# A head's sample outer products in one burst of four row tiles, and the first output chunk begun ahead of the last head's scores

## What is computed

```python
def _layer(h, pos, S0, ...):
    xn = _rmsnorm(h, norm_g)
    q, k, v, g_r, u, v_g, g_g = split(xn @ w_in)              # 7 x 1024 columns, 8 heads of 128
    q, k = rope(q), rope(k) * 128 ** -0.5
    o, S = retention(q, k, v, S0)    # per token: S = gamma_h * S + k^T v ; o = q S
    o = groupnorm(o) * silu(g_r)
    m = u * spatial_gate(layernorm(v_g)) * silu(g_g)
    return h + concat([o, m]) @ w_out, S, vn
```

## Time and profile before

| | us |
|---|---|
| median of 3 runs | 1172.91 (1171.78 to 1173.85) |
| the profiled execution | 1175.36 |
| span of its slowest core (core 2) | 1173.8 |
| spans of the eight cores | 1166.6 to 1173.8 |
| PE busy in that span | 1136.2 (97%) |
| DVE, POOL, ACT busy | 807.6, 661.8, 640.2 |

### The profile page before, as it was taken

How to read it: one execution, slowest core, us unless ns; L and a number is a source line. 1 busy time by engine, 2 the same in 40 slices (tenths; PEclk the granted TensorE clock), 3 DMA queues, 4 the chain that set the end, 5 groups by cost and what they waited for, 6 DMA issues and landing times.

```text
span 1173.8 us, 27480 instructions; the slowest of 8 cores (1166.6 to 1173.8 us)
## 1 busy us (share of the span) xinstructions
PE 1136.2 (97%) x9302; PEld 646.3 (55%) x9302; DVE 807.6 (69%) x1567; ACT 640.2 (55%) x1142; POOL 661.8 (56%) x696
## 2 busy tenths in 40 slices
PE   5899999999999999999999999999999999999997
PEld 2454456666666665544544445666666666664453
DVE  3864667776776777776574487776776776776864
ACT  4484566555555656524443488555655655663433
POOL 3346356567567666503475785567666666662332
PEclk9999999999999999999999999999999999999999
DMA  9731546456556466756791028256446447556543
GB/s 206 178 99 36 83 93 133 103 92 125 115 90 120 100 116 152 128 170 155 177 208 28 12 40 157 79 100 117 104 99 124 111 86 129 125 119 144 180 182 144
DMA packets 144489, 139.59 MB, mean 119 GB/s; under 512 B 41952, under 2 KB 115424, under 8 KB 144352
## 3 DMA queue, kind: packets, MB, share of 16 engines
q1 hardware_dynamic: 123088, 95.11, 29.0%
q0 software_dynamic: 21120, 42.48, 24.5%
q10 hardware_dynamic: 144, 0.26, 0.1%
HBM read 124.51 MB, written 43.19 MB: 143 GB/s over the span
## 4 chain that ended last, share of the span: by engine, by line
PE 85%; ACT 6%; issue 3%; DMA 3%; DVE 2%; POOL 1%; DVEq 0%; ACTq 0%; POOLq 0%; SPq 0%
PE ps L824 32%; PE ps L702 12%; PE ps L1233 10%; PE ps L868 9%; PE ps L633 5%; PE ps L1175 4%; ACT L483 2%; ACT B_q L483 1%; PE ps L903 1%; PE ps L949 1%; PE ps L1031 1%; PE ps L989 1%; PE ps L952 1%; PE ps L574 1%; DMA h<-hb_51 1%
## 5 line engine op out<-in xcount | busy, mean ns | idle before, releaser
L483 ACT ACTIVATE B_q<-ps 64x512 f32<-64x512 f32 x128 | 75.8, 592 | 98.7 <-DVE A_q L849 62.9
L483 ACT ACT_TABLE_LOAD x73 | 93.7, 1283 | 15.2 <-DVE rs L960 10.1
L840 POOL TENSOR_TENSOR kT_83<-A_k,B_k 128x512 bf16<-128x512 f32 x32 | 40.7, 1272 | 80.4 <-DVE B_k L838 80.4
L483 ACT ACTIVATE sq<-ps 128x512 f32<-128x512 f32 x64 | 38.2, 596 | 45.8 <-PE ps L952 45.0
L958 DVE TENSOR_TENSOR og<-ps,sgr_96 128x512 f32<-128x512 f32 x32 | 22.1, 692 | 59.1 <-ACT sq L483 59.1
L840 POOL TENSOR_TENSOR kT_84<-A_k,B_k 128x512 bf16<-128x512 f32 x32 | 41.1, 1283 | 28.8 <-DVE B_k L838 28.7
L958 DVE TENSOR_TENSOR og<-ps,sgr_97 128x512 f32<-128x512 f32 x32 | 22.1, 692 | 47.1 <-ACT sq L483 47.1
L1233 PE MATMUL ps<-TT,VV 128*128 128x512 bf16 x240 | 54.2, 379 | 0.0
L931 DVE SCALAR_TENSOR_TENSOR S32b<-S32b,ps 128x128 f32<-128x128 f32 x120 | 33.8, 282 | 18.7 <-PE ps L922 17.5
L999 POOL TENSOR_TENSOR VV<-s_100,sgg_99 128x512 bf16<-128x512 f32 x32 | 37.1, 1158 | 16.4 <-DVE kn_s L1063 11.6
L931 DVE SCALAR_TENSOR_TENSOR S32a<-S32a,ps 128x128 f32<-128x128 f32 x120 | 33.9, 282 | 17.8 <-PE ps L922 15.7
(11 more groups left out here) (674 smaller groups left out, 3505.8 us busy)
## 6 DMA issues: line engine op xcount, KB each, us to landing
stt_143<-st SPq DMA_DIRECT2D x16, 512.0 KB, 4.2
stt_142<-st SPq DMA_DIRECT2D x16, 512.0 KB, 4.8
ss_out<-stt_142 SPq DMA_DIRECT2D x16, 512.0 KB, 4.3
ss_out<-stt_143 SPq DMA_DIRECT2D x16, 512.0 KB, 3.7
cats<-catn_94 SPq DMA_DIRECT2D x14, 256.0 KB, 4.2
cats<-catn_95 SPq DMA_DIRECT2D x14, 256.0 KB, 3.4
hb_49<-xp SPq DMA_DIRECT2D x6, 512.0 KB, 4.2
hb_50<-xp SPq DMA_DIRECT2D x6, 512.0 KB, 4.0
```

The source lines that it names most:

```text
L483: P.add("act", lambda e: e.activation(out=out, in_=in_, func=func, **kw), r, w, t_act(n) + (0.2 if "accum_out" in kw else 0), tset=tset)
L840: pool(lambda e: e.tensor_tensor(out=dst[:], in0=A_k[:], in1=B_k[:], op=ALU.add), A_k.k() + B_k.k(), dst.k(), 512)
```

## The change

`s_kv` is no longer called once for each half. It becomes a generator that is begun once for each head, in quarter 2: it takes four banks, issues all four outer products in one operation, and holds back those banks that have not been summed yet, so that `brot` does not hand them out. Its first two sums and the write of half 0 stand in quarter 2, as before; the third stands behind `SC` in quarter 3, the fourth and the write of half 1 behind `OO` in quarter 3. The copy to `stb` becomes a step of its own (`s_stb`), half 0 in quarter 2 and half 1 in quarter 3 behind `s_o` of half 0. Behind the loop, the first four weight pairs of output chunk 0 are put ahead of `SC`, `GM` and `OO` of the last unit, in two banks of `brot` that are held back from these; the last `s_o` moves behind chunk 0's other three pairs and takes a bank of `tbank`.

```diff
@@ class Rot
+                self.items, self.i, self.held = list(items), 0, set()
             def __call__(self):
+                while True:
+                    x = self.items[self.i % len(self.items)]
+                    self.i += 1
+                    if x not in self.held:
+                        return x
@@ s_kv
-        def s_kv(l, h, half):
-            t = stt[half]
-            bs = (brot(), brot())
+        def s_kv(l, h):
+            bs = [brot() for _ in range(4)]
             def mm(e):
-                for j in range(2):
-                    p0 = (half * 2 + j) * 32
-                    r = e.matmul(ps[:, bs[j], :], kn_s[p0:p0 + 32, :], vmask[p0:p0 + 32].rearrange("p b v -> p (b v)"),
+                for j in range(4):
+                    r = e.matmul(ps[:, bs[j], :], kn_s[j * 32:j * 32 + 32, :], vmask[j * 32:j * 32 + 32].rearrange("p b v -> p (b v)"),
                                  start=True, stop=True)
                 return r
-            pe(mm, kn_s.k() + vmask.k(), [bk(b) for b in bs], 1.5 * MM)
+            pe(mm, kn_s.k() + vmask.k(), [bk(b) for b in bs], 2 * MM)
+            brot.held.update(bs)
             for j, b in enumerate(bs):
...
+                t, j0 = stt[j // 2], j % 2 * 4
+                dve((lambda t, j0, b: lambda e: e.scalar_tensor_tensor(
+                    out=t[:, j0:j0 + 4, :], in0=t[:, j0:j0 + 4, :], scalar=_C["gam"][h],
+                    in1=ps[:, b, :].rearrange("p (b v) -> p b v", b=4), op0=ALU.mult, op1=ALU.add))(t, j0, b),
+                    t.k((j0, j0 + 4)), t.k((j0, j0 + 4)) + [bk(b)], 512)
+                brot.held.discard(b)
+                if j % 2:
+                    half = j // 2
+                    dma("sp", ss_out[l, half * 8:half * 8 + 8, h].rearrange("b d v -> d b v"), t[:], t.k(), [("sso", l, h, half)], t.name, 524288)
+                yield
+
+        def s_stb(half):
+            act(stb[:], stt[half][:], AF.Copy, stt[half].k(), stb.k(), 1024)
+
+        def s_o(l, h, half, bank=None):
+            b = (bank or brot)()
@@ o_front
+        def o_front(l, c, a=0, b=7):
+            if a == 0:
+                obanks[c] = (orot(), orot())
+            o_mm(l, c, obanks[c], cat_ap(c), cat_k(c), 128, JO[a:b])
@@ the loop over units
                     SC(l, p)
+                if u.q == 3:
+                    next(kv)
...
                     OO(l, p, pp)
+                if u.q == 3:
+                    next(kv)
...
                 if u.q == 2:
-                    s_kv(l, h, 0)
+                    kv = s_kv(l, h)
+                    for t in range(2):
+                        next(kv)
+                    s_stb(0)
                     if h + 1 < H:
                         w_prep2(l, h + 1)
                 if u.q == 3:
                     s_o(l, h, 0)
-                    s_kv(l, h, 1)
+                    s_stb(1)
@@ behind the loop
+            first = [brot() for _ in range(5)]
+            orot.items, orot.i = first + [b for b in range(6) if b not in first], 0
+            o_front(l, 0, 0, 4)
+            brot.held.update(obanks[0])
             SC(l, p)
             GM(l, p)
             OO(l, p, pp)
-            s_o(l, H - 1, 1)
...
             for c in range(3):
-                o_front(l, c)
+                o_front(l, c, 4 * (c == 0))
+                if c == 0:
+                    s_o(l, H - 1, 1, tbank)
```

More of the change, by code:

```diff
@@ L469, in __init__ @@
             def __init__(self, items):
-                self.items, self.i = list(items), 0
+                self.items, self.i, self.held = list(items), 0, set()
             def __call__(self):
-                x = self.items[self.i % len(self.items)]
-                self.i += 1
-                return x
+                while True:
[3 more added lines that the diff above has]
+                        return x
         def pe(fn, r, w, dur, slack=0.0):
@@ L1188, in build_nc @@
         obanks = {}
-        def o_front(l, c):
-            obanks[c] = (orot(), orot())
-            o_mm(l, c, obanks[c], cat_ap(c), cat_k(c), 128, JO[:7])
+        def o_front(l, c, a=0, b=7):
+            if a == 0:
+                obanks[c] = (orot(), orot())
+            o_mm(l, c, obanks[c], cat_ap(c), cat_k(c), 128, JO[a:b])
         def o_chunk(l, c):
@@ L1401, in build_nc @@
             prot.items, prot.i = [6, 7, vbank.q[0]], 0
-            brot.items, brot.i = vbank.q[1:], 0
+            brot.items, brot.i, brot.held = vbank.q[1:], 0, set()
             w_prep2(l, 0)
@@ L1422, in build_nc @@
             wi = 15
+            kv = None
             for n in range(H * NQ):
```

## The result

The changed kernel takes 1162.49 us (median; the kernel before beside it 1173.38). The ratio of the two is **0.9897, 95% interval 0.9868 to 0.9926**. Ratios leave out disturbed executions and medians don't, so differences between kernels are taken from the ratios (0.001 is 1.2 us). The forecast was 1156 us, 0.9856 of the 1172.91 that it was worked out from, and the range 1151 to 1168: faster, as said, and inside the range, but 0.0041, about 5 us, short of the gain.

A forecast was written before the change was run, and what follows sets the result against it. TensorE, busy 1136.2 of 1173.8 us, was taken to bound the kernel. From the median 1172.91, less 11.6 for the heads and 5.9 for the layer ends, came 1155.4, given as 1156 us; range 1151 to 1168.

The forecast's parts named there:

- The burst costs 0.43 us: Four outer products on TensorE begin together and cost 0.43 us; bounds for 16 bursts 0 and 6.6 us of loss.
- ScalarE's order from the planner: Quarter 3: table load and silu go right behind `P_gr`, ahead of the `B_q` copies and squares; margin about 0.2 us.
- 0.83 us a head: Quarter 3 on TensorE: gain from the pair (0.42), until `P_k` (0.29) and ahead of `P_u` (0.15), less 0.01 and rounding.
- 14 x 0.83 = 11.6 us: Heads' total gain: seven heads a layer have a next one, 14 in all, 11.6 us.
- `KT` fits by 0.2 us, price 0: Quarter 3: fourth sum ends about 354.1, `KT` due in its bank at 354.38; cost 0, otherwise up to 8.4 us.
- The ends: 3.77 and 3.84 us, 5.9 together against the median: Layer ends: four early weight pairs cover the `qT_82` wait, no clock fall; 7.6 us from the profile, 5.9 by median.
- the weights are there, by a margin of 0.7 us: Layer end: the latest weights wanted early, `wo_2`, arrive at 492.05; their matmuls come no earlier than 492.8.
- the price 0 for the earlier write of half 1: Quarter 3: half 1's write is issued some 3 us earlier on SP, delaying nobody; cost 0.
- what is gained ahead of the output stage reaches the end: Output stage: TensorE hardly waits (0.3 us in all for its commonest line), so earlier gains reach the end.
- order kept: Rival: ScalarE keeps the silu behind the keys, `P_k` stays at 357.38, only the ends gain; 1167 us, chance 0.15.
- Banks bind: Rival: banks bind or the burst is half as good, about half the heads' gain left; 1161 us, chance 0.17.
- Ends unchanged: Rival: `qT_82` comes later than all cover, TensorE idles, the clock falls, only heads gain; 1161 to 1164, chance 0.06.

The follow-up runs named there:

- the double burst: Each burst of four outer products issued twice in a row, against the changed kernel: 1165.26 us in one execution.
- best version: Changed kernel, last head's second state write behind last transpose, residual chunks 2, 3 and `fing` loaded unwaiting, output-weight sums after last head's third sum: 1153.85 us, ratio 0.9835.
- the late write: Changed kernel with the last head's second state write issued behind the last transpose, in both layers: 1156.65 us, ratio 0.9847.

## Why the prediction was right, and where it wasn't

- **The burst costs 0.43 us**: right. Four show 0.39 us and the next matmul begins 0.32 later, as two did; the double burst adds 0.22.
- **ScalarE's order from the planner**, on a margin of 0.2 us: right, to the operation (table load at 349.19, right behind the end of `P_gr`). And the heads' gain needs it: taken back, nothing is left of it.
- **0.83 us a head**: right in mechanism, too small. A middle period fell by 1.04 (43.54 to 42.50). The three terms were 0.42 for the pair, 0.29 for the wait at `P_k` and 0.15 ahead of `P_u`; between starts of the trace I find the same. The 0.2 more are two passages that the sum didn't look at: in quarter 2 `OO` begins 1.98 us after the start of `P_gr` instead of 2.10, and `KV` begins 1.01 us after the start of the sample projections instead of 1.09. Why these two shrank isn't shown.
- **14 x 0.83 = 11.6 us**: 11.0 in the changed kernel (5.5 a layer). The middle periods gained more than forecast; the first head of layer 0 and the last of each layer gained less (0.83 and 0.63 from burst to burst in the best version), and in the changed kernel VectorE stands in front of the weight sums in the last head; without that it is 12.5 (best version). The term was mis-sized in both directions, and that it came out this near is partly luck.
- **`KT` fits by 0.2 us, price 0**: the price is right, the way to it only in part. On VectorE the fourth sum runs from 350.32 to 351.00, ahead of the end of `s_o`, as forecast; but the planner put `KT` behind `P_k`, at 353.05, 1.7 us later than forecast, so the narrow fit wasn't put to the test. With the four sums together VectorE does bind, for about 1.05 us a head.
- **The ends: 3.77 and 3.84 us, 5.9 together against the median**: the mechanism was right (no wait for `qT_82`, no fall of the clock at the layers' ends in any core of the changed kernel), and so is the size: on the median core the two output stages of the table shrink by 4.9 us in the changed kernel and by 5.9 once the late write is out of the way. In the changed kernel none of it that can be told from noise reached the slowest core. That the weights are there, by a margin of 0.7 us, held in the changed kernel, but not on every core with the late write, where core 2 waits 2.2 us for a pair.
- **The step that failed** is the price 0 for the earlier write of half 1 ("moved into time in which their queues have room, and nobody waits for them"). It is true of SP's queue in the middle of the heads. At a layer's end the same move puts 512 KB ahead of the 128 KB that the last transposes wait for, and behind these wait the residual's loads and `fing`. With it falls the sentence that what is gained ahead of the output stage reaches the end: that rested on waits of 0.3 us in the trace of before, where the stage began 3 us later against its loads. The forecast's miss is 0.0041 of the time before; moving that one write gives 0.9897 - 0.9847 = 0.0050, about 6 us, with intervals that lie apart.
- **Rivals**: *order kept* was put at 1167; as an experiment it came to 1171.7, since the heads became 3.2 us longer than before instead of staying equal. *Banks bind* didn't happen, and was one edit away. *Ends unchanged*, 1161 to 1164, is the rival whose number came out, by another mechanism than the one named; that the time still lies inside the range is owed to the range, which takes in this rival and others.

## To carry to other kernels

When an edit moves an operation earlier, follow its transfers through every queue to the place where the loop ends: a write that nobody waits for in the middle of a loop can stand ahead of one that everybody waits for at its end. A gain at the end of a stage counts only if the next stage's loads come earlier by as much; look up who holds them back. And a matmul taken away may pay only if the order on the engine that frees its bank changes too: here the removed pair gave nothing without the early silu, and the early silu nothing without the spread sums.

## What the hardware showed that I hadn't expected

How long a 128 KB write takes to land depended here on what was issued a few microseconds ahead of it, not on its size: from issue to transpose median 5.6 us before, 9.5 with 512 KB ahead of it on the same queue, 12.6 with three more loads beside it, 5.7 with the write moved; the last `cats` of a layer, just as large, takes 1.9 to 3.4 us in both kernels. In the stretch from 1040 to 1072 us of the changed kernel's core 2 (40 slices of 0.8 us; busy share of the DMA engines in tenths, then GB/s) the engines are busy in part and idle in part, from 1049.6 to 1052.0 and from 1057.6 on, while `cats`, issued at 1045.69, is still out until 1059:

```profile
DMA  9998998999930009818785000164006008999999
GB/s 184 195 174 159 143 148 163 271 311 215 90 12 11 12 12 106 28 12 166 153 192 177 4 1 0 35 137 156 0 4 155 5 0 189 343 328 358 343 230 118
...
ss_out<-stt_143 SPq DMA_DIRECT2D x1, 512.0 KB, 11.5
...
wo_7_76<-w_o POOLq DMA_DIRECT2D x1, 512.0 KB, 12.4
```

So it isn't bandwidth alone. The Trainium skill (DMA: Bandwidth & Descriptors, Queues, rings and completion order) says that a DMA engine takes the descriptors of one queue in order and reports a transfer as complete only after all earlier writes of that engine, of other queues too. The rows agree with it in that `ss_out` (11.5 us from issue to landing), the weights `wo_7` (12.4) and `cats` (13.6 to its transpose) are all late together. Why the engines stand idle meanwhile no run here shows.

Left open too: why only some cores wait for late loads (above all 2 and 4 in layer 1, 0 and 6 in layer 0 of the profiled execution), and the wait of 1.5 us for a step of VectorE some 115 us into layer 0's output stage, which the kernels with the changed ends have and those with the old ends don't (0.3 there).
